# Gate and up projection of a two-block layer stack: half of its contraction by seven products instead of eight, with weight sums from GpSimd and tokens on the partitions

## The reference

```python
        h = rmsnorm(x, g_ffn[i])
        gu = h @ w_ffn_gu[i]
        g, u = jnp.split(gu, 2, axis=-1)
        x = x + (jax.nn.silu(g) * u) @ w_ffn_down[i]

        ple_gate = jax.nn.sigmoid(rmsnorm(x, g_ple[i]) @ w_ple_gate[i])
        x = x + ple_gate * (p[i] @ w_ple_proj[i])
```

## Time and profile before

| | before |
|---|---|
| median of 3 runs | 2905.14 us (2904.03 to 2905.32) |
| the profiled execution | 2904.31 us, span 2902.5 us |
| PE busy | 2878.8 us (99% of the span), 15902 matmuls |
| PEld busy | 2482.2 us (86%) |
| DVE busy | 2054.3 us (71%) |
| ACT busy | 1360.5 us (47%) |
| POOL busy | 417.2 us (14%) |
| DMA | 520.71 MB, mean 179 GB/s; the weight queue 56.5% of 16 engines' span |
| granted TensorE clock | full in all 40 slices |

### The profile page before, as it was taken

One profiled execution on the slowest core, in us unless ns is written; L12 is line 12 of the kernel. 1 busy time (PEld: TensorE's weight loads), 2 busy tenths in 40 slices (PEclk: granted clock), 3 DMA queues, 4 the chain that ended last, 5 costly groups with the idle time before them and its releaser, 6 DMA issues.

```text
span 2902.5 us, 42029 instructions
## 1 busy us (share of the span) xinstructions
PE 2878.8 (99%) x15902; PEld 2482.2 (86%) x15902; DVE 2054.3 (71%) x2296; ACT 1360.5 (47%) x1618; POOL 417.2 (14%) x392
## 2 busy tenths in 40 slices
PE   9999999999999999999999999999999999999999
PEld 7888888888888888888888888888888888888887
DVE  6666667875786677765666667876887766787766
ACT  6555544346654444443343344544444545434553
POOL 1000000104020000000000000013950100791010
PEclk9999999999999999999999999999999999999999
DMA  6555566654466566666555565566555554655555
GB/s 218 174 173 166 169 188 186 211 156 138 130 197 188 186 201 200 190 190 192 175 181 188 184 192 188 176 189 195 176 180 168 159 184 151 181 170 182 171 160 174
DMA packets 467294, 520.71 MB, mean 179 GB/s; under 512 B 17720, under 2 KB 414123, under 8 KB 466888
## 3 DMA queue, kind: packets, MB, share of 16 engines
q1 hardware_dynamic: 462240, 509.68, 56.5%
q0 software_dynamic: 4080, 6.30, 0.8%
q10 hardware_dynamic: 824, 2.69, 0.3%
HBM read 516.49 MB, written 2.12 MB: 179 GB/s over the span
## 4 chain that ended last, share of the span: by engine, by line
PE 60%; DVE 8%; ACT 3%; issue 2%; DMA 0%; POOL 0%; ACTq 0%; DVEq 0%; SPq 0%
PE PG L2250 34%; PE PG L2253 17%; DVE WL L1331 3%; PE PG L2282 3%; PE PG L2284 3%; PE PG L2283 3%; ACT WH L658 1%; DVE G L1344 1%; DVE G L1650 0%; DVE MIX L1767 0%; DMA RAW<-in_w_ffn_gu_dram 0%; PE PX L2360 0%; ACT L899 0%; DVE F L1344 0%; PE PX L2303 0%
## 5 line engine op out<-in xcount | busy, mean ns | idle before, releaser
L1331 DVE TENSOR_TENSOR WL<-RAW,WH 128x1024 fp32r<-128x1024 f32 (+1 forms) x956 | 1152.8, 1232 | 514.3 <-ACT WH L658 497.8
L658 ACT ACTIVATE WH<-RAW 128x1024 fp32r<-128x1024 f32 (+1 forms) x972 | 995.9, 1050 | 808.9 <-PE PG L2253 410.0
L2250 PE MATMUL PG<-XH,WH 128*128 128x512 f32 x3712 | 1172.3, 397 | 7.8 <-DVE WL L1331 4.1
L2253 PEld LDWEIGHTS PG<-XH,WL 128*128 128x128 f32 x3712 | 697.3, 188 | 164.7
L2250 PE MATMUL PG<-YH,WH 128*128 128x512 f32 x2336 | 737.1, 397 | 1.3 <-DVE WL L1331 1.2
L2253 PE MATMUL PG<-XH,WL 128*128 128x256 f32 x3712 | 729.5, 278 | 0.0
L2250 PEld LDWEIGHTS PG<-XH,WH 128*128 128x128 f32 x3712 | 566.3, 189 | 12.1 <-DVE WL L1331 5.3
L2253 PEld LDWEIGHTS PG<-YH,WL 128*128 128x128 f32 x2336 | 438.8, 188 | 103.8
L2253 PE MATMUL PG<-YH,WL 128*128 128x256 f32 x2336 | 459.0, 278 | 0.0
L2250 PEld LDWEIGHTS PG<-YH,WH 128*128 128x128 f32 x2336 | 356.0, 189 | 6.4 <-issue 3.3
L2282 PE MATMUL PG<-WH,XH 128*128 128x512 f32 x576 | 228.0, 396 | 0.8 <-DVE WL L1331 0.8
(11 more groups left out here) (301 smaller groups left out, 2069.5 us busy)
## 6 DMA issues: line engine op xcount, KB each, us to landing
RAW<-in_w_in_dram SPq DMA_DIRECT2D x488, 512.0 KB, 4.5
RAW<-in_w_ffn_gu_dram SPq DMA_DIRECT2D x176, 512.0 KB, 4.6
RAW<-in_w_ffn_down_dram SPq DMA_DIRECT2D x88, 512.0 KB, 4.5
RAW<-in_w_out_dram SPq DMA_DIRECT2D x64, 512.0 KB, 4.4
RAW<-in_w_rnn_out_dram SPq DMA_DIRECT2D x40, 512.0 KB, 4.5
RAW<-in_w_attn_out_dram SPq DMA_DIRECT2D x32, 512.0 KB, 4.6
RAW<-in_w_o_dram SPq DMA_DIRECT2D x32, 512.0 KB, 4.6
RAW<-in_w_ple_gate_dram SPq DMA_DIRECT2D x32, 512.0 KB, 4.8
```

What stands on the lines that cost most here:

```text
L658: nc.scalar.activation(WH[:, u % SLOTS, 0:nk, :], RAW[:, u % SLOTS, 0:nk, :], ACT.Copy)\
L1331: V_.tensor_tensor(WL[:, u % SLOTS, 0:nk, :], RAW[:, u % SLOTS, 0:nk, :], WH[:, u % SLOTS, 0:nk, :].bitcast(fp), ALU.subtract).then_inc(s. ...
L2250: mm(PG[:, 2 * par + j, :], WH[:, slot, kk, P * j:P * j + P], x, start=grp.opens and n == 0 and kk == 0, stop=False)
L2253: last = mm(PG[:, 2 * par + j, T:2 * T], WL[:, slot, kk, P * j:P * j + P], x[:, 0:T], start=False, stop=grp.closes and n == len(units) - 1 ...
```

## The change

The contraction of gate and up is cut into eight steps of 256 rows, each with 512 gate and 512 up columns, so a step needs two wide units: one gate unit and one up unit. There are 11 such groups, 4 in `gu0`, 4 in `gu1` and 3 in `gu2`. Steps 1, 3, 5 and 7 are made as in `rows_group`, with 24 matmuls of 512 columns. Steps 0, 2, 4 and 6 take the two token halves, the two row blocks and gate and up as 2x2 blocks and form seven products instead of eight, with 21 matmuls of 512 columns. They need sums of the weights and of the activations:

- `sums` on GpSimd makes, from two raw units, one subtraction of 128x1024 and two of 128x512.
- `sum_high` (ScalarE) and `sum_low` (VectorE) split the two 128x1024 sums into high and low parts; of the up unit only half is still split as a weight (`half_high`, `half_low`).
- `post_fold_pairs` replaces `post_fold` in `w_o` and makes the sums of the activations once.
- The seven products have one PSUM bank each; the eighth, `TURN`, takes transposes. There is no second set of banks.
- `outer_sums` and `last_sum` (VectorE) add the products up, `gates_tanh` and `gate_pairs` make the hidden features with tokens on the partitions, `turn_hidden` turns them on TensorE, and `hidden_high` and `hidden_low` split them into `XH`.
- SyncE's load into a slot of a seven-product step also waits for `tsum`, the end of GpSimd's sums of that step.
- `w_o` and `gu` are written out instead of looped. The projection of `p` moves from `down1` to `down2`, the bias strip from `gu0` to `down2`, the bias tiles from `gu1` to `conf0`.

```diff
@@ SyncE
+                    if c.var is None and u - SLOTS in sums_due:
+                        sp.wait_ge(s.tsum, sums_due[u - SLOTS])
@@ GpSimd
+            def sums(k, gate):
+
+                up = gate + 1
+                for u in (gate, up):
+                    pool.wait_ge(raw_sems[u % SLOTS], 16 * (u // SLOTS + 1))
...
+                if k:
+                    pool.wait_ge(s.tlo, 2 * k - 1)
+                nc.gpsimd.tensor_tensor(two512(SUMS[:, 0, :]), two512(b), both, ALU.subtract).then_inc(s.tsum, 1)
+                pool.wait_ge(s.tsum, 2 * k + 1)
+                if k:
+                    pool.wait_ge(s.tlo, 2 * k)
+                nc.gpsimd.tensor_tensor(SUMS[:, 1, 0:512], b[:, 512:1024], SUMS[:, 0, 0:512], ALU.subtract)\
+                    .then_inc(s.taps, 1)
+                pool.wait_ge(s.taps, k + 1)
+                nc.gpsimd.tensor_tensor(SUMS[:, 1, 512:1024], SUMS[:, 1, 0:512], a[:, 512:1024], ALU.subtract)\
+                    .then_inc(s.tsum, 1)
+                pool.wait_ge(s.tsum, 2 * k + 2)
@@ ScalarE
+            def sum_high(part):
+
+                k = c.n.get("tsum", 0) // 2
+                c.add("tsum")
+                act.wait_ge(s.tsum, 2 * k + part + 1)
+                if k:
+                    act.wait_ge(s.tunit, 2 * k - 1 + part)
+                nc.scalar.activation(SUM_H[:, part, :], SUMS[:, part, :], ACT.Copy).then_inc(s.thi, 1)
@@ VectorE
+            def sum_low(part):
...
+                dve.wait_ge(s.thi, 2 * k + part + 1)
+                V_.tensor_tensor(SUM_L[part], SUMS[:, part, :], SUM_H[:, part, :].bitcast(fp), ALU.subtract)\
+                    .then_inc(s.tlo, 1)
+            def half_low():
+
+                u = c.n["unit"]
+                dve.wait_ge(s.hi, c.value("unit", 1))
+                V_.tensor_tensor(WL[:, u % SLOTS, 2:4, :], RAW[:, u % SLOTS, 2:4, :],
+                                 WH[:, u % SLOTS, 2:4, :].bitcast(fp), ALU.subtract).then_inc(s.lo, 1)
+                c.add("unit")
+            def four(grp, n):
+                split(grp, slice(2 * n, 2 * n + 1))
+                sum_low(0)
+                sum_low(1)
+                half_low()
+            def outer_sums():
+
+                seen, g = c.value("seen", DC), c.n.get("pairs", 0) + 1
+                dve.wait_ge(s.tunit, DC // 2 * g)
+                from_act()
+                done(V_.tensor_tensor(U2, GATE[0], P6, ALU.add))
+                done(V_.tensor_tensor(U3, U2, P7, ALU.add))
+                dve.wait_ge(s.unit, seen - 1)
+                read_p(V_.tensor_tensor(GATE[0], GATE[0], P2, ALU.add))
+                read_p(V_.tensor_tensor(GATE[1], U3, P4, ALU.add))
+                dve.wait_ge(s.fifth, g)
+                done(V_.tensor_tensor(U2, U2, P5, ALU.add))
+                read_p(V_.tensor_tensor(UP[1], U3, P5, ALU.add))
+            def gate_pairs(b):
+
+                from_act()
+                done(V_.scalar_tensor_tensor(GATE[b], Tf[:, b, :], 1.0, GATE[b], ALU.add, ALU.mult))
+                V_.scalar_tensor_tensor(GATE[b], GATE[b], der(BOTH + b), UP[b], ALU.mult, ALU.mult)\
+                    .then_inc(s.gated, 1)
+            def gu(body, before, following, then, first, last):
+
+                for m, grp in enumerate(body):
+                    for n in range(DC // 2):
+                        if n % 2 == 0:
+                            four(grp, n)
+                            if n == 0 and m:
+                                outer_sums()
+                            if n == 2 and m:
+                                gate_pairs(0)
+                        else:
+                            split(grp, slice(2 * n, 2 * n + 1))
+                            if n == 1 and m:
+                                last_sum()
...
+                            if n == 3 and m:
+                                gate_pairs(1)
+                            split(grp, slice(2 * n + 1, 2 * n + 2))
...
+                        if m and n >= 6:
+                            hidden_low(m - 1, n - 6)
@@ TensorE
+            def product(to, x, hi, lo, start, stop):
+                mm(to, x[:, 0:P], hi, start=start, stop=False)
+                mm(to, x[:, P:T], hi, start=False, stop=False)
+                return mm(to, x[:, 0:P], lo, start=False, stop=stop)
```

More of the change, by code:

```diff
@@ new lines, in gu @@
+            def gu(body, before, following, then, first, last):
+                for m, grp in enumerate(body):
+                    for n in range(DC // 2):
+                        if n % 2 == 0:
+                            four(grp, n)
+                            if n == 0 and m:
+                                outer_sums()
+                            if n == 2 and m:
+                                gate_pairs(0)
+                        else:
+                            split(grp, slice(2 * n, 2 * n + 1))
+                            if n == 1 and m:
+                                last_sum()
+                            if n == 1 and not m:
+                                for job in before:
+                                    job()
+                            if n == 3 and m:
+                                gate_pairs(1)
+                            split(grp, slice(2 * n + 1, 2 * n + 2))
+                        if first and m == 0 and n == 4:
+                            rms_columns()
+                        if m and n >= 6:
+                            hidden_low(m - 1, n - 6)
+                units = len(following.units())
+                split(following, slice(0, 2))
+                outer_sums()
+                split(following, slice(2, 3))
+                last_sum()
+                split(following, slice(3, units))
+                gate_pairs(0)
+                gate_pairs(1)
+                split(then, slice(0, 1))
+                ahead[0] = units + 1
+                TURNS[:] = [TURN, P1]
+                for b in range(NB):
+                    hidden_low(len(body) - 1, b)
+                TURNS[:] = [TURN, TURN]
@@ L2444, in after_gu1, with turn_hidden @@
                     for h in (2 * j, 2 * j + 1):
-                        mm(PX[:, 2 + h % 2, :], FLIP, MIXf[:, 512 * h:512 * h + 512], start=True, stop=True)\
+                        mm(PX[:, 2 + h % 2, :], FLIP, STAGE[:, 512 * h:512 * h + 512], start=True, stop=True)\
                             .then_inc(s.flip, 1)
+            def turn_hidden(b, to):
+                pe.wait_ge(s.gated, c.next("gated"))
+                if c.n["turned"] and to is TURN:
+                    pe.wait_ge(s.op, c.n["turned_from"] + c.n["turned"])
+                c.add("turned")
+                for q in range(4):
+                    last = nc.tensor.transpose(to[:, P * q:P * q + P], GATE[b][:, P * q:P * q + P], IDENT)
+                last.then_inc(s.hidden, 1)
@@ L2607, in _ @@
             for ph in phases:
[L2608 to L2609 removed]
+                if ph.name[:2] == "gu":
+                    for m, grp in enumerate(ph.body):
+                        pairs_group(m, ph.fresh.get(m, ()), ph.name == "gu0")
+                    pe.wait_ge(s.read_p, 4 * c.n["pairs"] - 1)
                     continue
@@ L2618, in turn @@
                             mid = {0: lambda: turn_pairs(4), 1: lambda: turn_pairs(6)}
+                        if ph.name[:4] == "down" and j == 0 and first:
+                            mid = {1: last_hidden_p if ph.name == "down2" else last_hidden}
                         if ph.name[:3] == "dil":
```

406 lines of the change are left out of this document (309 added, 97 removed).

## The result

The change takes 3053.86 us, the median of 4 runs (3051.54 to 3056.78), against 2905.23 us before: a ratio of 1.051 (1.049 to 1.053). The forecast was 3022 us, in a range of 2955 to 3090, with slower at 92%. The sign and the range held; the loss of 149 us is 31 us more than the 118 us that were forecast.

The account below looks back on a forecast made before the run. The prediction took TensorE's stream to bound the gate and up stretches (busy 491.65 of 492.00 us). It added 112 us for the loop, 2 for the edges and 4 for `down2` to 2904.3, giving 3022 us, range 2955 to 3090.

Parts of the forecast that it names:

- TensorE's stream: Gate and up stretches: fewer matmuls save 41.8 us, 88 transposes add 10.3; 31.5 us gained if TensorE stayed the bound.
- The closed loop: Gate and up: load, GpSimd's sums, ScalarE's and VectorE's splits, next load; a pair of steps takes 12.7 us, not 10.2.
- GpSimd's 128x512 operation, taken at 1.30 us: First 512-column sum of a seven-product step, sized by the least multiplication of that size in the earlier profile.
- The loop's sum, +112: Gate and up: 11 groups of 54.8 us, with +4 us each for VectorE's jobs, make 603 us against 490.6.
- the edges, +2 (-10 and +12): Gate and up phases: waits for `outer_sums` at three ends +12 us, sums ready early at three starts -10.
- `down2`, +4 us (0 to 12): Projection of `p` moved here: VectorE's 9.3 us per group against TensorE's 9.8, plus round trips to ScalarE.
- `w_o`, 0 (0 to 8): VectorE's larger job, some 10.5 us of 11.15 per group, was taken as covered by TensorE's stream.
- `conf0`, 0 (0 to 4): The six tile copies, 4.1 us, move here from the gate and up phases; taken to cost nothing.
- The rival of no mutual hold-up: Gate and up: GpSimd and VectorE do not delay each other; a pair 11.56 us, a group 46.4, 2930 us; 6%.
- The rival that pauses cost more than their length: TensorE at group starts: half clock after each pause, 4.8 us more per group, 52 us in all, 3074 us; 12%.
- my own signs of being wrong: A pair at 10.2 us, GpSimd's operations at 2.4 and 1.3 throughout, clock below full, or time in `w_o`, `down2` or `conf0`.
- the 14,900 to 15,200 forecast: Sign expected in the profile after: TensorE with about that many matmuls instead of 15902.

Follow-up runs that it names:

- small_sums: The change with GpSimd's three subtractions cut to 32 columns each, same number, places and waits, rest of the sums zero; 2900.21 us (one run).
- half_first: The change with the half split of the up unit put before the splits of the two sums; 3012.18 us, 1.037 to the kernel before.
- no_pp: The change with the projection of `p` left out of `down2`; 3025.31 us (one run).
- memsets: The change with GpSimd's three subtractions replaced by fills of about the same length, same places and waits; 2981.88 us (one run).
- two_dve: The change with seven products only in steps 0 and 4, sums made by VectorE, half split first; 2943.89 us, 1.013 to the kernel before.

## Why the prediction was right, and where it was off

- **TensorE's stream** (31.5 us to gain if it stayed the bound): right in its pace. `small_sums` ran it at 41.9 us a group, against 459.1 / 11 = 41.7. Of the 31.5 us it kept 22 (490.6 to 468.5); the ends take the rest.
- **The closed loop** through load, GpSimd, ScalarE and VectorE: right in every member and their order; `half_first` shows the place of the load in it, `small_sums` that nothing else of the change binds. In the group looked at, the pair with L664 undisturbed and without jobs took 12.93 us against 12.7, the others 13.78 to 15.62; a group 56.4 against 54.8.
- **GpSimd's 128x512 operation, taken at 1.30 us, "the one that was not held up"**: this term was mis-sized. L664 took 1.79 us in the mean, 0.49 more: about 2.15 in 24 of its 44 cases, as beside the split above, and the forecast's 1.3 in 16, as at 1259.21. (The second such operation, L667, I had drawn with its hold-up, 3.80 to 6.05; it took 2.13.) The row that I should have gone by stood in the earlier trace rows too, whose median is 2.35. I had drawn one hold-up of GpSimd in a pair; in more than half of the pairs there are two.
- **The loop's sum, +112, and the edges, +2 (-10 and +12)**: 11 groups of 56.4 us are 620.7 us, 130 over the stream's 490.6, so the loop is 18 short; the term above makes 44 x 0.49 = 21.6. The three phases take 619.2, so the edges are -1.5, within their bounds (at the three ends TensorE waits 1.2 us each for `outer_sums`, not 3.7). What I left out helped: gu before held 9.5 us of other work (500.1 less 490.6), most of it the strip and the tile copies that moved away.
- **`down2`, +4 us (0 to 12)**: outside its bounds. It rose by 26.8 us, of which 11.2 is TensorE's moved work, so +15.6; `down1` fell by 10.1 instead of 11.2. This is the term that was furthest out: I had summed VectorE's work to 9.3 us against TensorE's 9.8 and let it hide, but a sum of work says nothing of its order. TensorE waited 1.5 us in each pair for a split that stood behind the round trip to ScalarE, and a pair took 11.75 us. `no_pp` shows the projection as the cause.
- **`w_o`, 0 (0 to 8)**: 3.0 us, within its bounds, but by the hold-ups and not by VectorE's larger job. It is TensorE's wait for the first low part of `gu0` (3.09 us, to 1108.93), and that is late because a VectorE job of the last group of `w_o` met GpSimd's first sum:

```profile
1098.16 2.40 POOL L660 TENSOR_TENSOR RT<-RAW 128x1024 f32<-128x1024 f32 x1 [194.51 <-DMA RAW<-in_w_ffn_gu_dram]
1098.28 2.83 DVE L1827 SCALAR_TENSOR_TENSOR XRES<-G,XRES 128x512 f32<-128x512 f32 x1
```

  In `small_sums` and `memsets` the phase takes 89.2 us, as before. **`conf0`, 0 (0 to 4)**: 5.2 from there on, a little over its bound. **`down0`, `down1`**: 1.0 us each; 0.9 are the eight transposes of the last group, which I had counted to the stream. **`ple`**: 2.7 us for which I had no term; TensorE waits 2.3 us for splits there.
- **The rival of no mutual hold-up** (2930 us): wrong, as forecast. `memsets` prices the hold-ups at 72 us; without them the kernel took 2982 us, not 2930, since a group still took 49.5 us against this rival's 46.4. The Trainium skill (SBUF — State Buffer, section "SBUF: two separate sides") has GpSimd and VectorE take turns for a whole instruction where VectorE reads two SBUF operands and GpSimd reads SBUF; splits of 1508 ns beside subtractions and 1223 beside fills agree.
- **The rival that pauses cost more than their length** (3074 us, 12%): its mechanism occurs, and with it one of my own signs of being wrong, a granted clock below full. Behind a pause of 5.94 us in the changed kernel the clock was at 0.50 from 1266.4 to 1269.0, and the mean in gu was 0.92 to 0.94. How much of this reached the time no run measured. Little, I think, because the pair of 12.93 us came out near its 12.7 without any term for the clock, and TensorE has slack behind each pause. Where TensorE is the bound, as in `two_dve`, the clock shows in the time.
- **Whether the change does what it says**: yes, 15158 matmuls against 15902, within the 14,900 to 15,200 forecast.

In sum: gu came to +119 against my +114, and that it lies so near is in part luck, since three errors nearly cancel (+18, -3.5 and -9.5). The 31 us missing are `down2` with `down1` (16.7 against 4), gu 5, `conf0` and on 5, `w_o` 3, `ple` 2.7, and `down0` 1, with 1 us in small pieces. So the time lies in part in `down2` and `conf0`, which I had named as a sign of being wrong.

## What to carry to other kernels

Before work is handed to an idle engine, write down the closed loop it will stand in (buffer free, load, each engine, buffer free) and compare its length, not any engine's busy share, with the stage's pace; 31% free on VectorE and all of GpSimd said nothing here. Where two engines hold each other up, the idle one is not free: in the same order of work the sums were cheaper on the busy VectorE (2930 us) than on the idle GpSimd (3012 us). And take away the new work's cost in one run (small operations, same places) early: it showed that even nearly free sums would have gained 5 us, as other moves of the change had spent the gain. A margin of work (9.3 us against 9.8) does not hide a chain of hand-overs in it.

## What the runs showed of the hardware

- GpSimd's fills of 128x1024 take 956 ns and do not hold VectorE up (splits at 1223 ns); its subtractions from SBUF do (splits at 1508 ns, and its own 128x512 operations at 1793 and 2132 ns, where the least multiplication of that size in the earlier trace rows has 1296).
- Moved under GpSimd's subtractions, a VectorE operation of 0.68 us took 1.82 us in the mean (`half_low` in `half_first`), and one of 0.69 us 2.83 (L1827 at 1098.28 in the changed kernel).
- In `two_dve`, after 2.12 and 0.47 us of idling, TensorE's matmuls started 0.43 us apart at a granted clock of 0.50 until about 1255.5, though it had been busy for 43 us before the first pause. The group start before it (pauses of 2.12 and 0.21 us, to 1205.43) shows 0.50 too, from 1204.5 to 1207. In the changed kernel, after 2.12 and 0.54 us before 1225.54 and 1227.70, the window from 1228 to 1232 shows 1.00. I did not find what makes the two kernels differ.
